# Two transformer blocks on one core: operand buffers placed at chosen addresses modulo 256 bytes

## What is computed

```python
# first block
h = rmsnorm(x, g_mlp[l])
hid = jnp.square(jax.nn.relu(jnp.einsum("bsd,df->bsf", h, w_mlp_in[l])))   # 1024 -> 4096
x = x + jnp.einsum("bsf,fd->bsd", hid, w_mlp_out[l])                       # 4096 -> 1024
...
# second block, four times, 1024 -> 2816 -> 1024
def swiglu(x, w1, w3, w2):
    return (jax.nn.silu(x @ w1) * (x @ w3)) @ w2
...
# second block, once: gated mixer, 2048 + 2048 columns
z = jax.nn.gelu(x @ w_in, approximate=False)
u, v = jnp.split(z, 2, axis=-1)
...
return (u * mixed.reshape(B, S, SGU_HALF)) @ w_out
```

## Time and profile before

| | |
|---|---|
| time, median of 3 runs | 1520.36 us (1519.9 to 1523.21) |
| the profiled execution's own time | 1522.35 us |
| its span from the first to the last instruction | 1520.5 us |
| mean granted TensorE clock | 0.985 |
| PE busy | 1469.3 us, 97% of the span |
| PEld busy | 1341.2 us, 88% |
| DVE, ACT, POOL busy | 929.7, 659.0, 95.8 us |
| moved from memory and back | 268.43 MB, mean 177 GB/s |

### The profile page before, as it was taken

The page is one execution under the profiler, slowest core; times in us unless marked ns, Lnnn a source line. Parts: engine busy times, 40 slices in busy tenths (PEclk is TensorE's granted clock), DMA queues, the critical chain, the costliest instruction groups (busy, mean ns, idle before and its releaser), DMA issues.

```text
span 1520.5 us, 25321 instructions
## 1 busy us (share of the span) xinstructions
PE 1469.3 (97%) x10475; PEld 1341.2 (88%) x10484; DVE 929.7 (61%) x1363; ACT 659.0 (43%) x834; POOL 95.8 (6%) x78
## 2 busy tenths in 40 slices
PE   8998998999999999999999999999999998999997
PEld 6988987899899999999789999999999876799996
DVE  5877357555665555657875555646555647765556
ACT  5655534333433334545244334425333448543332
POOL 0012141000020000100020000100000100100000
PEclk9999998999999999999999999999999999999999
DMA  7443344776577555655355555667555430465551
GB/s 257 145 137 100 137 140 153 218 216 218 179 239 259 194 190 183 197 182 191 115 199 189 190 182 185 202 199 234 194 191 182 156 113 29 139 205 185 192 193 56
DMA packets 191526, 268.43 MB, mean 177 GB/s; under 512 B 5740, under 2 KB 164752, under 8 KB 191182
## 3 DMA queue, kind: packets, MB, share of 16 engines
q1 hardware_dynamic: 186336, 250.05, 50.0%
q0 software_dynamic: 4224, 15.91, 3.1%
q10 hardware_dynamic: 878, 1.21, 0.3%
HBM read 261.92 MB, written 4.19 MB: 175 GB/s over the span
## 4 chain that ended last, share of the span: by engine, by line
PE 84%; DVE 9%; ACT 3%; DMA 2%; issue 1%; POOL 0%; DVEq 0%; ACTq 0%
PE bank L730 82%; PE bank L753 2%; DVE split L1981 2%; DMA ring<-in_ffn_w 2%; ACT split L1510 1%; DVE resid L2058 1%; DVE resid L2066 1%; DVE stats L2037 1%; DVE resid L2035 1%; DVE arena L2530 1%; ACT act_out L1532 0%; DVE arena L2573 0%; DVE stats L1995 0%; DVE arena L2178 0%; ACT gain_rows L1636 0%
## 5 line engine op out<-in xcount | busy, mean ns | idle before, releaser
L730 PE MATMUL bank<-hT_hi,split 128*128 128x256 f32 (+1 forms) x3984 | 720.5, 281 | 7.5 <-ACT act_out L1648 5.4
L1981 DVE TENSOR_TENSOR split<-ring,split 128x2048 fp32r<-128x2048 f32 x212 | 484.2, 2286 | 375.2 <-ACT split L1510 369.9
L730 PEld LDWEIGHTS bank<-hT_hi,split 128*128 128x128 f32 (+1 forms) x3984 | 617.4, 189 | 17.0 <-issue 10.8
L1510 ACT ACTIVATE split<-ring 128x2048 fp32r<-128x2048 f32 (+1 forms) x224 | 426.9, 1907 | 360.0 <-PE bank L730 321.4
L730 PE MATMUL bank<-hT_lo,split 128*128 128x256 f32 (+1 forms) x1992 | 559.1, 281 | 0.0
L730 PEld LDWEIGHTS bank<-hT_lo,split 128*128 128x128 f32 (+1 forms) x1992 | 377.1, 189 | 2.3
L730 PE MATMUL bank<-split,hid_hi 128*128 128x512 f32 x992 | 288.7, 397 | 0.0
L730 PEld LDWEIGHTS bank<-split,hid_hi 128*128 128x128 f32 x992 | 182.6, 188 | 40.8 <-issue 0.8
L730 PE MATMUL bank<-split,hT_hi 128*128 128x256 f32 (+1 forms) x896 | 179.1, 298 | 7.2 <-DVE split L1981 4.4
L730 PE MATMUL bank<-split,hid_lo 128*128 128x512 f32 x496 | 159.6, 395 | 0.0
L730 PEld LDWEIGHTS bank<-split,hT_hi 128*128 128x128 f32 x896 | 143.5, 190 | 15.9 <-issue 5.7
(11 more groups left out here) (212 smaller groups left out, 965.5 us busy)
## 6 DMA issues: line engine op xcount, KB each, us to landing
ring<-in_ffn_w SPq DMA_DIRECT2D x132, 1024.0 KB, 5.1
ring<-in_w_in SPq DMA_DIRECT2D x19, 1024.0 KB, 5.2
ring<-in_w_mlp_in SPq DMA_DIRECT2D x16, 1024.0 KB, 6.3
ring<-in_w_mlp_out SPq DMA_DIRECT2D x16, 1024.0 KB, 5.0
ring<-in_sgu_w_in SPq DMA_DIRECT2D x16, 1024.0 KB, 5.4
ring<-in_sgu_w_out SPq DMA_DIRECT2D x8, 1024.0 KB, 4.8
ring<-in_kv_w SPq DMA_DIRECT2D x6, 1024.0 KB, 5.4
ring<-in_w_out SPq DMA_DIRECT2D x4, 1024.0 KB, 4.9
```

The costliest lines, as they stand in the source:

```text
L730: ins = pe.matmul(o, lhsT, rhs, start=start, stop=stop)
L1510: act.activation(halves(q, n)[0], ring[:, u % SLOTS, 0:n], ACT.Copy).then_inc(hi_ready, 1)
L1981: dve.tensor_tensor(lo, ring[:, u % SLOTS, 0:n], hi.bitcast(F32), ALU.subtract).then_inc(split_ready, 1)
```

## The change

No instruction, wait, transfer or size of a transfer changes. The built programs have the same 10,858 instructions in the same order on every engine, and differ in addresses alone. A helper `place` puts an unused gap ahead of a buffer so that it starts at a chosen offset modulo 256. `arena` (of which `two` is the first part) and `split` move up ahead of the small rows, and `arena` grows by 96 bytes.

```diff
-ARENA = 14472
+ARENA = 14496
+LINE = 256
...
+        def place(offset):
+
+            base = -(-nc.sbuf_base // 32) * 32
+            gap = (offset - base) % LINE
+            if gap:
+                sb(f"gap{base}", [P, gap // 4])
+
...
+        place(128)
         ring = sb("ring", [P, SLOTS, UNIT])
         resid = sb("resid", [P, NB, D])
         xn = sb("xn", [P, NB, D])
...
+        place(64)
         with nc.sbuf_tensor("shared_rows", [P, 3 * MLP_BODY * 512], F32) as shared_rows:
             pass
         hid = sb("hid", [P, MLP_BODY, 512])
         hid_hi = sb("hid_hi", [P, MLP_BODY, 2, S], F32R)
         hid_lo = sb("hid_lo", [P, MLP_BODY, 2, S], F32R)
         hid_tok = hid[:, 2, :].rearrange("p (b c) -> p b c", b=NB)
+        place(128)
+        with nc.sbuf_tensor("arena", [P, ARENA], F32) as arena:
+            pass
+        two = sb("two", [P, 2, KT, S], F32R)
+        sb("arena_rest", [P, ARENA - 2 * KT * S])
+        place(192)
+        split = sb("split", [P, SPLIT, 2, UNIT], F32R)
+        place(128)
         const = sb("const", [P, N_CONST])
...
-
-        with nc.sbuf_tensor("arena", [P, ARENA], F32) as arena:
-            pass
-        two = sb("two", [P, 2, KT, S], F32R)
-        sb("arena_rest", [P, ARENA - 2 * KT * S])
-
...
-        split = sb("split", [P, SPLIT, 2, UNIT], F32R)
```

## The result

The changed kernel takes 1499.74 us (median of 4, 1498.6 to 1503.2) beside 1521.43 for the kernel before (4 runs, 1519.9 to 1523.21). The ratio is 0.9861, 95% interval 0.984 to 0.9882.

A forecast was written before the change was run, and what follows sets the result against it. PE's matmul pace was taken to bound the kernel. Terms of -2.0, -0.4, -0.4 and -0.1 us summed to -2.9, so 1520.36 us became 1517.5 us, with an 80% range of 1508 to 1528.5.

The forecast's parts named there:

- What bounds the kernel: PE is busy 97% of the span and 84% of the chain; DVE (61%) and ACT (43%) have slack.
- Term 2: 5952 matmuls of `hT` over `split`, distance -32 to +64: taken as 0; bounds named were losses of 6.0 or 9.5 us.
- the floor: Best pace seen for split products, 116.7 ns per 256 columns, 8% over plain bf16, shared by three distances.
- Term 1: 1200 matmuls of `split` over `hT`, distance +32 to -64: 118.3 to 116.7 ns, saving 2.0 us.
- The part on `su`: Stretch at 672.20 us, no longer following a slow one: 383 matmuls save 1.1 ns each, 0.4 us.
- Term 3: 240 matmuls of `two` over `split`, distance +32 to +64: at the floor, saving 0.4 us.
- 512-wide part: Down products (+32 to 128) and the few from `two`: taken as 0, with a loss bound of 2.5 us.
- Term 4: Roundings and transfers: ACT's rounding into `split` from 1916 ns to near 1.90 us, saving 0.1 us.
- The long term goes wrong: Rival, chance 0.24: `hT` over `split` at +64 is slow like +32, giving 1527.9 us, or 1524.4 at 117.8 ns.
- The floor gives way: Rival, chance 0.20: a new distance removes the 8%, down products first: 1494 us; all about 1427, partial 1508.
- Distance does nothing: Rival, chance 0.12: the pattern is chance, or gains and losses cancel, giving 1520.4 us.
- My remark on `su`: `su` ran at 117.8 ns despite distance -32, so a pace can be carried on from the products before.

The follow-up runs named there:

- experiments 1 and 2: 1: kernel before, only a 96-byte gap ahead of `split`, 1498.38 us. 2: changed kernel's buffer order with the old offsets, 1522.26 us.
- Experiments 10 and 14: 10: changed kernel with `hid` at 192 instead of 64, 1513.17 us. 14: that plus a 256-column bf16 matmul ahead of feed-forward units following down products, 1504.18 us.
- experiment 12: Changed kernel with `hT_lo` and every low half in `split` 32 bytes further: 1528.49 us, one run.
- experiments 11 and 13: 11: changed kernel, `ring` alone at 0 instead of 128, 1498.93 us. 13: kernel with `hid` at 192 plus 64-column bf16 matmuls ahead of feed-forward units, 1519.7 us.
- Experiments 4 to 8: Changed kernel with `split` at 64, 128, 0, 160, 224 instead of 192: 1516.66, 1534.16, 1532.2, 1529.29, 1531.93 us, one run each.

## Why the prediction was wrong

**What bounds the kernel** held: PE's pace is the time, and 22.0 us less of PE busy are 21.9 us less of span.

**Term 2 is the step that failed.** I wrote that at the floor the long products' term is 0 and took the 512-wide row at +64 for proof that the floor holds there. The runs showed about -18 us in its place: at +64, 256-wide products take 113.4 ns. The 512-wide row didn't carry over. The paces of 512-wide products follow another order of distances (229.0 at -64, 226.5 at 0, 232.5 at 128), and at 0 the two widths are at opposite ends. A floor that three distances share was an observation, and I used it as a bound for an untried one. My words that the only slow rows are at +32 also passed over the 117.8 ns of `su` at -32. The range of this term should have reached below 0.

**Term 1** had its direction and was too large: in `sv`, `split` over `hT` went from 118.3 to 117.8 ns and not to 116.7. Over all its successive starts the mean went from 118.9 to 117.7 ns, because a few stretches reached 113.3: 1200 x 1.2 = 1.4 us in place of 2.0. The part on `su`, 0.4 us, was too small. It went from 117.8 to 113.3 ns, 380 x 4.4 = 1.7 us. **Term 3** was too small: of three long stretches one is at 117.8 and two are at 113.3, where 116.7 was taken, and the mean over all starts went from 118.9 to 115.2 ns, 240 x 3.7 = 0.9 us in place of 0.4. Its 512-wide part, taken as 0, gained 1488 x 0.5 = 0.7 us. **Term 4** promised 0.1 us from roundings near 1.90 us, and they didn't get shorter: 1920 ns for 1916.

**The rivals.** "The long term goes wrong" took the neighbour +32 for a guide to +64. The neighbour is slow indeed, 118.4, but the price jumps within 32 bytes. "The floor gives way" is what came, at a chance of 0.20, though not where it was priced first. It was to be the down products, farthest apart, which hardly moved. "Distance does nothing" is refuted by experiments 1 and 2. The Trainium skill states on the page "SBUF — State Buffer", section "Who interferes with whom", that PE has two read ports, for the moving operand and for weight loads, which are independent, and that it never waits on anyone. By that rule the place of `split` would do nothing. The traces do not agree, and the measurement decides: the pace of `hT` over `split` goes from 113.4 to 120.0 ns with the place of `split` alone. That ACT and DVE don't slow PE's matmuls agrees with the earlier trace rows.

**My remark on `su`**, that a pace can be carried on, pointed at something that mattered more than I made of it. Experiments 10 and 14 show that the pace of `hT` over `split` depends on what runs ahead, with the same addresses for both. How it is passed on isn't shown.

**What stays open.** What inside PE or SBUF meets was not seen: experiment 12 refuted the simple reading by the next weights and left the other unproved in size. Which of the two paces a stretch at distance 64 gets can't be told ahead: in experiments 11 and 13 stretches changed it though neither their own operands nor what stands right ahead of them had changed. Experiments 4 to 8, 12 and 14 rest on one execution each. Steps under 32 bytes weren't tried.

## What to carry to other kernels

Where PE bounds a kernel in float32r and its pace per column is some per cent over the plain one, try the stationary and the moving operand at a few different distances modulo 256 bytes and measure; here one gap of 96 bytes was worth 1.4%, and the kernel with the worst distance, 0, took 2.3% more time than the changed one (one run). Read the pace from windows inside a stretch, never from mean durations, and look at each kind of product for itself: a distance that is good for one width may be bad for another. A pace that several cases share is not a bound for an untried case, and where a pace depends on the products ahead, price whole sequences and not pairs.

## What the runs showed of the hardware that was not expected

Steady paces of 256-column float32r matmuls come in few values: 113.3, 116.7, 117.3, 117.8, 118.3, 118.7 and 120.0 ns, and 119.0 where the low halves stood apart. At 2.4 GHz the first of them is 272 cycles, the second 280 and the 120.0 is 288, which is 256 plus 16, 24 and 32. None comes to the 108 of plain bf16. At a distance of 64, of either sign, there are two, 113.3 and 117.8, and a stretch keeps the one it begins with: 383 matmuls in a row do in `su`. -32 has two as well (116.7 and 117.8), and so have +96 and 128. A foreign bf16 matmul of 256 columns ahead of a unit changed which one the loops have. One of 64 columns didn't, though `su` and the keys and values changed with it.
